# Seven products of blocks in the attention's output projection, two of its 19 low parts on GpSimd

## The reference, cut to what matters

```python
def reference(x, ...):                       # D = 2048, 256 rows
    xn = rmsnorm(x, norm_gain[0])
    q, k, v, gate = split(xn @ attn_w_in)    # 2048 x 8192
    o = diff_attention(q, k, v)              # 8 heads, softmax, bias by distance
    o = rmsnorm_per_head(o) * head_gain * (1 - lambda_init)
    x = x + (o * silu(gate)) @ attn_w_out    # 2048 x 2048, the stage of this change
    xn = rmsnorm(x, norm_gain[1])
    a, g, z = split(xn @ conv_w_in + b_in)   # 2048 x 6144
    u = layernorm(depthwise_conv(a * sigmoid(g), 31 taps))
    x = x + (silu(u) * silu(z)) @ conv_w_out + b_out
    return rmsnorm(x, final_gain)
```

## Time and profile before

| | us |
|---|---|
| median of 3 runs | 823.15 |
| lowest, highest | 823.1, 823.22 |
| the profiled execution | 823.21 |
| its span in the profile | 821.4 |
| TensorE busy | 813.1 |
| VectorE busy | 660.0 |
| ScalarE busy | 460.3 |
| GpSimd busy | 236.3 |

### The profile page before, as it was taken

One profiled execution on the slowest core, in us unless ns is written; L12 is line 12 of the kernel. 1 busy time (PEld: TensorE's weight loads), 2 busy tenths in 40 slices (PEclk: granted clock), 3 DMA queues, 4 the chain that ended last, 5 costly groups with the idle time before them and its releaser, 6 DMA issues.

```text
span 821.4 us, 13877 instructions
## 1 busy us (share of the span) xinstructions
PE 813.1 (99%) x5614; PEld 752.1 (92%) x5614; DVE 660.0 (80%) x1111; ACT 460.3 (56%) x600; POOL 236.3 (29%) x115
## 2 busy tenths in 40 slices
PE   9999999999999999999999999999999999999996
PEld 9988899889998899888888899999999999998885
DVE  6578794797658784798788987999999999569782
ACT  7756643647336543656554455455664555597562
POOL 0400010000000000002000008989889888680000
PEclk9999999999999999999999999999999999999999
DMA  9995599966654556534656556556556555556842
GB/s 329 394 385 184 184 284 359 309 184 205 216 192 153 172 195 217 189 117 154 218 192 205 191 176 229 188 191 198 192 177 205 176 187 202 180 209 228 310 149 102
DMA packets 104137, 175.22 MB, mean 213 GB/s; under 512 B 3808, under 2 KB 41200, under 8 KB 103536
## 3 DMA queue, kind: packets, MB, share of 16 engines
q1 hardware_dynamic: 99712, 163.65, 58.2%
q0 software_dynamic: 2720, 8.39, 4.5%
q10 hardware_dynamic: 1648, 2.40, 0.8%
HBM read 172.30 MB, written 12.09 MB: 224 GB/s over the span
## 4 chain that ended last, share of the span: by engine, by line
PE 94%; DMA 3%; SPq 1%; ACT 1%; DVE 1%; issue 0%; ACTq 0%
PE ps_acc L1404 16%; PE ps_acc L1406 16%; PE ps_acc L1407 16%; PE ps_acc L1390 13%; PE ps_acc L1392 13%; PE ps_acc L1393 13%; DMA sb_xs<-in_x 2%; DMA sb_w_raw<-in_attn_w_in 1%; SPq L386 1%; SPq L388 1%; PE ps_a L1366 0%; PE ps_d L1494 0%; PE ps_d L1492 0%; PE ps_a L1506 0%; PE ps_a L1508 0%; PE ps_d L1493 0%
## 5 line engine op out<-in xcount | busy, mean ns | idle before, releaser
L536 ACT ACTIVATE sb_w_hi<-sb_w_raw 128x2048 fp32r<-128x2048 f32 x142 | 271.3, 1919 | 210.9 <-PE ps_acc L1407 140.1
L927 DVE TENSOR_TENSOR sb_w_lo<-sb_w_raw,sb_w_hi 128x2048 fp32r<-128x2048 f32 x97 | 220.3, 2289 | 80.5 <-ACT sb_w_hi L536 80.1
L491 POOL TENSOR_TENSOR sb_w_lo<-sb_w_raw,sb_w_hi 128x2048 fp32r<-128x2048 f32 x45 | 208.0, 4630 | 253.2 <-ACT sb_w_hi L536 253.2
L1404 PE MATMUL ps_acc<-sb_conv_hi,sb_w_hi 128*128 128x256 f32 x768 | 213.1, 277 | 0.0
L1407 PE MATMUL ps_acc<-sb_conv_hi,sb_w_lo 128*128 128x256 f32 x768 | 212.2, 276 | 0.0
L1406 PE MATMUL ps_acc<-sb_conv_lo,sb_w_hi 128*128 128x256 f32 x768 | 212.2, 276 | 0.0
L1162 DVE SCALAR_TENSOR_TENSOR ps_d<-sb_uT,sb_dwT,ps_d 128x256 f32<-128x256 f32 x480 | 189.0, 493 | 4.5 <-ACT ps_d L779 4.5
L1390 PE MATMUL ps_acc<-sb_w_hi,sb_act_hi 128*128 128x512 f32 x384 | 149.7, 390 | 0.0
L1392 PE MATMUL ps_acc<-sb_w_lo,sb_act_hi 128*128 128x512 f32 x384 | 149.6, 390 | 0.0
L1393 PE MATMUL ps_acc<-sb_w_hi,sb_act_lo 128*128 128x512 f32 x384 | 149.4, 389 | 0.0
L1406 PEld LDWEIGHTS ps_acc<-sb_conv_lo,sb_w_hi 128*128 128x128 f32 x768 | 144.2, 188 | 0.0
(11 more groups left out here) (210 smaller groups left out, 891.0 us busy)
## 6 DMA issues: line engine op xcount, KB each, us to landing
sb_w_raw<-in_attn_w_in SPq DMA_DIRECT2D x59, 1024.0 KB, 7.0
...
sb_w_raw<-in_attn_w_out SPq DMA_DIRECT2D x16, 1024.0 KB, 5.0
sb_w_raw<-in_conv_w_in SPq DMA_DIRECT2D x16, 1024.0 KB, 5.0
sb_w_raw<-in_conv_w_out SPq DMA_DIRECT2D x15, 1024.0 KB, 5.1
weight_sums<-in_conv_w_out POOLq DMA_DIRECT2D x6, 1024.0 KB, 11.3
sb_w_raw<-weight_sums SPq DMA_DIRECT2D x4, 1024.0 KB, 5.8
...
```

Source lines behind the costliest of these rows:

```text
L491: pool.tensor_tensor(w_part(w_lo, c), w_raw[c % RING][:], w_part(w_hi, c).bitcast(F32), ALU.subtract).then_inc(lo_ready_pool, 1)
L536: act.activation(w_part(w_hi, c if like is None else like), w_raw[slot][:], ACT.Copy).then_inc(hi_ready, 1)
L927: dve.tensor_tensor(w_part(w_lo, like), w_raw[slot][:], w_part(w_hi, like).bitcast(F32), ALU.subtract).then_inc(lo_ready, 1)
L1404: pe.matmul(into, left_hi, hi[:, kt], start=(kt == 0 and f % 2 == 0), stop=False, skip_group_check=True)
```

## The change

The attention's output projection takes the list `OUT_CHUNKS` too: 19 chunks in place of 16, with 12 whole chunks of 24 matmuls and seven products of 12. All chunks of the conv move up by three places in the count, so their places in the ring turn by three. The function `two_groups` on TensorE now serves both projections. New on the engines in this stage:
- ScalarE: `fill_acc` copies the rows of x of groups 1 and 2 into `acc` (the products then add to them), `m_scale` scales the 8 tiles of `mT` that the sums need in place, `m_sum_high` makes five high parts of sums, `copy_m_bank` copies a bank of PSUM three times;
- VectorE: five sums of activation blocks, five low parts of them, and the additions of groups 1 and 2 in six single pieces, since the products end at different times;
- GpSimd's queue: eight transfers that make the weight sums of this projection, ahead of the eight for the conv's;
- low parts: GpSimd makes those of (0, 3) and (2, 1) (`POOL_AMONG`), VectorE the other 17;
- the first pair: the load, the high and the low part of its chunk 7 go ahead of the second half of x, its squares and the norm's factor.

```diff
+POOL_AMONG = [CHUNKS_ATT + OUT_CHUNKS.index(what) for what in ((0, 3), (2, 1))]
...
-                        if first and t == 1 and i in (1, 2):
-                            st = i - 1
+                        if first and t == 1 and i in (1, 3):
+                            st = i // 2
...
                 if st == 0:
-                    high_part(RING + 2, 2, 2)
+                    for i in (2, 3):
+                        high_part(RING + i, i, 2)
...
+            def fill_acc(n):
+                act.wait_ge(acc_free, 2 * (G_OUT + n + 1))
+                for st in range(ST):
+                    act.activation(acc[:, 2 * (n % 2) + st], xs[:, st, n * GW:(n + 1) * GW], ACT.Copy
+                                   ).then_inc(x1_filled, 1)
...
+            m_high(3)
+            hi_after((0, 0))
+            fill_acc(1)
+            hi_after((0, 1))
+            m_scale(2)
+            hi_after((0, 2))
+            m_scale(3)
+            hi_after((0, 3))
+            fill_acc(2)
+            for n, i in enumerate((S3, S0, S4, S6, S2)):
+                m_sum_high(n, i)
+            squares(0)
+            hi_after((1, 0))
+            copy_m_bank(T1, 0)
+            hi_after(T1)
+            x1_high(0)
+            hi_after((1, 1))
...
+            hi_after(T3)
+            squares(1)
+            act.wait_ge(acc_free, 4 + 2 * (G_OUT + 3))
+            x1_high(1)
+            hi_after((3, 0))
+            squares(2)
+            x1_high(2)
+            hi_after((3, 1))
...
+            low_after((0, 2))
+            a11, a12, a21, a22 = m_rows()
+            dve.wait_ge(m_scaled, 8)
+            dve.tensor_tensor(m_raw_sums[S3], a12, a11, ALU.subtract).then_inc(m_sum_ready, 1)
...
+            add_rows(0)
+            low_after((0, 3))
+            for n, i in enumerate((S3, S0, S4, S6, S2)):
+                m_sum_low(n, i)
+            low_after((1, 0))
+            x1_turn(0)
+            low_after(T1)
+            x1_low(0)
...
+            low_after(T4)
+            product_done(dve, T4, att_chunk)
+            dve.wait_ge(x1_copied, 3)
+            dve.tensor_tensor(x1_of(1, 1), acc[:, 3], m_partial[2], ALU.subtract).then_inc(acc_free, 1)
+            x1_turn(1)
+            low_after(B22)
```

More of the change, by code:

```diff
@@ new lines, in _ @@
+            copy_m_bank(T2, 1)
+            hi_after(T2)
+            hi_after((2, 1))
+            copy_m_bank(B12, 2)
+            hi_after(B12)
+            hi_after(T4)
+            hi_after(B22)
+            hi_after(T3)
[6 more added lines that the diff above has]
+            hi_after((3, 1))
+            hi_after((3, 2))
+            squares(3)
+            hi_after((3, 3))
@@ L1148, in _ @@
+            x1_low(1)
+            low_after((3, 0))
+            x1_turn(2)
+            low_after((3, 1))
+            x1_low(2)
+            low_after((3, 2))
+            add_rows(3)
+            x1_turn(3)
+            low_after((3, 3))
             x1_low(PAIRS - 1)
@@ L1524, in _, with times @@
                 pair_slot(PAIRS - 1, i)
-            for i in range(NCH * PAIRS):
-                c, n = CHUNKS_ATT + i, i // NCH
-                if i < NCH:
-                    pe.wait_ge(m_split, CK * (i + 1))
+            def times(c, into, left, start=False):
                 low_part_ready(pe, c)
-                if i % NCH == 0:
-                    pe.wait_ge(acc_free, 2 * (G_OUT + n + 1))
-                project(c, i % NCH, n % 2, act_hi, act_lo)
+                high, low = w_part(w_hi, c), w_part(w_lo, c)
+                for k in range(CK):
+                    pe.matmul(into, left[0][:, k], high[:, k], start=start and k == 0, stop=False,
+                              skip_group_check=True)
+                    pe.matmul(into, left[0][:, k], low[:, k], start=False, stop=False, skip_group_check=True)
+                    ins = pe.matmul(into, left[1][:, k], high[:, k], start=False, stop=(k == CK - 1),
+                                    skip_group_check=True)
+                ins.then_inc(w_free, 1)
@@ new lines, in own, with two_groups, rows @@
+            def own(c, n, i, hi, lo):
+                low_part_ready(pe, c)
+                project(c, i, n % 2, hi, lo, filled=True)
+            def two_groups(chunk_of, hi, lo, sums, bank_copied):
+                def rows(st, a):
+                    return [part[:, 8 + a * CK:8 + (a + 1) * CK, st * P:(st + 1) * P] for part in (hi, lo)]
+                own(chunk_of((1, 0)), 1, 0, hi, lo)
+                times(chunk_of(T1), bank_a[1][:], rows(0, 0), start=True)
+                own(chunk_of((1, 1)), 1, 1, hi, lo)
+                times(chunk_of(B21), acc[:, 2], sums(S3))
+                if chunk_of is att_chunk:
+                    pe.wait_ge(x1_filled, 4)
+                else:
+                    pe.wait_ge(y_ready_pre, 6)
+                own(chunk_of((2, 0)), 2, 0, hi, lo)
+                pe.wait_ge(bank_copied, 1)
+                times(chunk_of(T2), bank_a[1][:], sums(S0))
+                own(chunk_of((2, 1)), 2, 1, hi, lo)
+                pe.wait_ge(bank_copied, 2)
+                times(chunk_of(B12), bank_a[1][:], sums(S4))
+                times(chunk_of(T4), acc[:, 3], sums(S6))
+                times(chunk_of(B22), acc[:, 0], sums(S2))
+                times(chunk_of(T3), bank_a[0][:], rows(1, 1), start=True)
@@ L1609, in _ @@
             pe.wait_ge(y_ready_pre, 2)
[L1610 to L1623 removed]
+            two_groups(out_chunk, conv_hi, conv_lo, sums, copied)
             for st in range(ST):
```

258 lines of the change are left out of this document (157 added, 101 removed).

## The result

| kernel | median, us | lowest | before, same chip | ratio to before, 95% interval |
|---|---|---|---|---|
| changed | 839.01 | 838.63 | 823.15 | 1.0191, 1.0173 to 1.0209 |

The changed kernel is 1.9% slower. The forecast was 837.2 with a range of 833.5 to 841.0, so the time lies inside it, 1.8 us above the forecast. The profiled execution took 838.63 us, its span is 836.8. One of the six executions of the changed kernel took 4710.88 us and one of the kernel before 829.51; the ratio leaves both out and goes by medians of 838.85 and 823.15.

A forecast was written before the change was run, and what follows sets the result against it. TensorE was taken to bound the kernel, with VectorE near its limit in the changed stage. Waits of 17.65 us less 2.72 give +14.9; 823.2 - 0.87 + 14.9 = 837.2 us, range 833.5 to 841.

The forecast's parts named there:

- What bounds it: TensorE bounds the kernel, busy 813.1 of 821.4 us; in the changed stage VectorE is near its limit, slack 12.2 us.
- Term 1: TensorE's work in the output projection: eight block products become seven, 84 matmuls in place of 96, -2.72 us.
- Term 2: First pair: chunk 7's load, high and low part go earlier, so TensorE's wait there goes, -0.87 us.
- Term 3: Output projection to the conv's fourth chunk: VectorE's work grows from 75.1 to 86.7 us, against TensorE's 84.6.
- rival (d): In the changed stage VectorE never waits, so the kernel is not slower: 822.3 us, chance 0.04.
- Term 4: Same stretch laid end to end: TensorE waits ahead of chunks 8, 9, 10, 20 and 22, 17.65 us in sum.
- Rival (b): GpSimd's low part of chunk 10 contends with VectorE's of chunk 11, +2.3 us: 839.5 us, chance 0.10.
- Rival (c): TensorE's clock falls to 1.2 GHz at the 5.1 us wait, up to 5.4 us more: 838 to 842.6, chance 0.13.
- What I said would prove me wrong: No waits on GpSimd, waits in the conv behind its fourth chunk, or the granted clock leaving 1.00 in the stage.
- Queues: Eight more transfers for weight sums, ahead of the conv's eight, cost TensorE 0, with a bound of 1.0 us.

The follow-up runs named there:

- e7: Changed kernel with ScalarE's and VectorE's order in the stage rewritten and five low parts on GpSimd in place of two: 819.90 us.
- e10: e7 with the first pair as before the change: 819.84 us.
- e1: Kernel before with only the first pair's edit (its chunk 7 ahead of the second half of x and its squares): 822.41 us.
- e11: e7 run again, beside e10 on the same chip: 819.57 us.
- e8: e7 with two low parts on GpSimd in place of five, those of chunks 3 and 11: 829.73 us.
- e5: Changed kernel as it is, run again on another occasion: 839.34 us.
- e2: Changed kernel with the low part of chunk 10 moved from GpSimd to VectorE: 837.16 us.
- e3: Changed kernel with extra products keeping TensorE busy in its waits ahead of chunks 9, 10, 20 and 22: 838.08 us.
- e9: Changed kernel with 18 extra products on TensorE in the wait ahead of chunk 22 alone: 839.12 us.

## Why the prediction was right, and where not

- **What bounds it.** Right. VectorE had 12.2 us of slack in the stage, the change spent it, and TensorE waits at the five places laid out and, in the first trace, nowhere behind. In six other traces of this order it waits once more in the conv, 0.3 to 0.4 us.
- **Term 1, -2.72.** Right in size; e7 shows it as 2.72.
- **Term 2, -0.87.** The mechanism was right: high 7 and low 7 are done before the statistics, and the wait goes. The second half of x came 1.8 us later (its squares at 37.40 against 35.62), not 2.7, and nothing waited for it. The size was wrong: it came from one execution, whose first loads were 0.8 us later than in e10. Measured are 0.35 (e1) and 0.27 (e10, e11), each below what those runs can tell from nothing.
- **Term 3, VectorE's sum of 86.7.** The window shows 89.7, of which 2.8 are low 11 beside GpSimd. No run shows the floor itself, a VectorE with this sum that never waits. The nearest is e8: with 86.7 us of work in a better order the kernel is 0.9% slower than before. In its trace VectorE is busy 86.4 of the 94.1 us from chunk 3 to chunk 22; an estimate from these, 829.7 less the idle 7.7, is 822.0, near the 822.3 of rival (d). With three low parts less the kernel is faster than before.
- **Term 4, the waits.** Laid 2.0, 3.9, 3.3, 3.3, 5.1; the list has 1.2, 3.7, 0.5, 3.3, 3.4. Chunk 8: ScalarE's fill and small highs take 1.06 and 0.52 from start to start, not 1.2 and 0.54, and the squares are shorter. Chunk 10 and chunk 22: TensorE was not idle but slow. Chunk 9 at half rate ends 2.4 us later (12 x 0.2), which is taken from chunk 10's wait; chunk 20 at half rate takes 1.7 from chunk 22's. That the total still came out follows from VectorE's chain, which set the end: `x1_low(3)` was laid to end at 495.6 on the clock of before, which is 494.5 with the stage 1.1 us earlier, and it ended at 494.56. That it is so near is in part luck: the chain was 0.3 us ahead at low 14 and lost this at idle times that were not laid (0.86 ahead of low 15, 0.25 ahead of low 16), and e5 of the same kernel has 0.5 us more up to `x1_low(3)`. Behind it came the third slow stretch, 1.65 us, which is the distance from 837.2 to the profiled 838.63 but for 0.2; the 0.2 is that the start brought 1.14 us in this trace and not 0.87.
- **Rival (b), contention, 0.10.** The mechanism is there, and the row it was read against could not show it. The Trainium skill, GPSIMD Engine Reference, section 1 (Specifications), was right in its rule that VectorE instructions with two SBUF inputs contend with GpSimd. The traces agree (5.12 against 2.29). The price was put in the wrong place: GpSimd's low 10 took 4.73 us, 0.1 more, and VectorE's low 11 paid 2.8. That fell on VectorE's idle time ahead of low 14 (laid 3.3, measured 0.69, and still more than 0, so the 2.8 did not move low 14). In e2 the chain to `x1_low(3)` is 0.9 to 1.4 us shorter; there low 10 is also ready 2.2 us sooner and low 14 starts 0.7 sooner, so how much of this is the collision by itself stays open.
- **Rival (c), the clock, 0.13.** Here the working failed. The earlier trace rows shows the clock at 1.00 for 5 us after the last matmul at the kernel's end, and I took waits under 5 us as safe. The clock fell to 1.2 GHz at waits of 3.7, 3.3 and 3.4 us. The row was one execution: over the thirteen traces the clock falls 2.1 to 5.2 us after the last matmul, so the 5 us were no bound. The Trainium skill, TensorE: Matmul & The Clock Gate, section Why this matters for your kernels, says that gaps of some us between bursts bring the slow clock back; these traces agree in eleven of fifteen waits of 3.2 us and more that were not filled (the table under e3, and e8), and show that it is not so each time. Its cost is small here, 0.2 to 1.4 us. That two of the three slow stretches end in a wait which another engine sets would explain this, but e9, which was to show it, leaves it open.
- **What I said would prove me wrong.** The granted clock did leave 1.00 in the stage, and the idle time ahead of low 14 did not come. A wait in the conv behind its fourth chunk came as well, 0.3 to 0.4 us in six traces. The forecast of 837.2 held, in part by luck, because the first was mostly covered and the idle time ahead of low 14 was filled by the slow low 11, which cost the chain nothing there.
- **Queues.** Eight more transfers of sums cost nothing that TensorE saw: e7 has them all and no wait.
